# The mixing stage of a hybrid layer: S5 rows loaded and gated first, tiles combined in every other row

## The reference, cut to what matters

```python
w_den = jax.nn.softmax(jnp.stack(lses, axis=0), axis=0)              # 3 groups, per position and head
attn = jnp.einsum('gbsh,gbshd->bshd', w_den, jnp.stack(outs, axis=0))
y_a = attn.reshape(b, s, 512) @ w_attn_proj[l]

y_s = jax.nn.gelu(s5_ssm(...))
y_s = y_s * jax.nn.sigmoid(y_s @ w_glu[l] + b_glu[l])
y_b = y_s @ w_ssm_proj[l]

mixed = jax.nn.sigmoid(gate_a) * y_a + jax.nn.sigmoid(gate_b) * y_b
```

## Time and profile before

| | before |
|---|---|
| median of 3 runs | 5241.57 us (5239.97 to 5242.58) |
| the profiled execution | 5241.3 us, its span 5239.6 us |
| granted TensorE clock over the span | 0.972 |
| TensorE busy | 4959.3 us, 95% of the span |
| VectorE busy | 2979.8 us, 57% |
| ScalarE, GpSimd busy | 1723.3 us, 871.9 us |

### The profile page before, as it was taken

The page is one execution under the profiler, slowest core; times in us unless marked ns, Lnnn a source line. Parts: engine busy times, 40 slices in busy tenths (PEclk is TensorE's granted clock), DMA queues, the critical chain, the costliest instruction groups (busy, mean ns, idle before and its releaser), DMA issues.

```text
span 5239.6 us, 78307 instructions
## 1 busy us (share of the span) xinstructions
PE 4959.3 (95%) x29176; PEld 4413.7 (84%) x29176; DVE 2979.8 (57%) x5537; ACT 1723.3 (33%) x2719; POOL 871.9 (17%) x561
## 2 busy tenths in 40 slices
PE   8999999997689979896999999999999999999998
PEld 6888888886579967685999999999999999999997
DVE  4343331003746666354656666656677777777776
ACT  4121111111246731132333333333334444344443
POOL 0000000002212001133111322213222121222221
PEclk9999999998789989997999999999999999999999
DMA  3222221312244444543454554645566666666665
GB/s 131 77 71 76 88 76 69 113 70 76 42 152 145 148 155 144 173 130 123 168 175 161 170 179 158 202 160 179 181 221 216 222 216 223 240 228 228 226 216 192
DMA packets 254790, 814.55 MB, mean 155 GB/s; under 512 B 33692, under 2 KB 66199, under 8 KB 218136
## 3 DMA queue, kind: packets, MB, share of 16 engines
q1 hardware_dynamic: 218776, 693.78, 36.9%
q0 software_dynamic: 30096, 98.23, 7.7%
q10 hardware_dynamic: 5760, 20.45, 1.2%
HBM read 659.68 MB, written 154.71 MB: 155 GB/s over the span
## 4 chain that ended last, share of the span: by engine, by line
PE 48%; DVE 3%; issue 1%; ACT 0%; DMA 0%; POOL 0%; POOLq 0%; DVEq 0%; ACTq 0%
PE ex_g L2130 31%; PE ex_d L2144 15%; DVE ex_wdl L2237 1%; PE ex_g L2116 1%; DVE ex_xl L2244 1%; ACT ex_xh L2196 0%; DVE ex_at L2267 0%; DVE ex_t L2258 0%; DVE ex_t L2265 0%; DMA ex_nxt<-slots_d 0%; DVE ex_ath L2270 0%; POOL ex_y L2085 0%; DMA ex_xg<-h_d,ex_nxt 0%; DVE ex_y L2285 0%; POOL out L2088 0%
## 5 line engine op out<-in xcount | busy, mean ns | idle before, releaser
L2130 PE MATMUL ex_g<-ex_xh,ex_wgh 128*128 128x256 f32 (+2 forms) x4352 | 1282.9, 295 | 13.7 <-DVE ex_xl L2244 7.4
L2130 PE MATMUL ex_g<-ex_xh,ex_wgl 128*128 128x256 f32 (+2 forms) x4352 | 1276.6, 293 | 0.0
L2130 PE MATMUL ex_g<-ex_xl,ex_wgh 128*128 128x256 f32 (+2 forms) x4352 | 1276.2, 293 | 0.0
L2130 PEld LDWEIGHTS ex_g<-ex_xh,ex_wgh 128*128 128x128 f32 x4352 | 815.8, 187 | 44.0 <-DVE ex_xl L2244 22.0
L2130 PEld LDWEIGHTS ex_g<-ex_xl,ex_wgh 128*128 128x128 f32 x4352 | 816.0, 188 | 7.6
L2130 PEld LDWEIGHTS ex_g<-ex_xh,ex_wgl 128*128 128x128 f32 x4352 | 817.2, 188 | 0.0
L2183 ACT ACTIVATE ex_wgh<-ex_wg 128x2048 fp32r<-128x2048 f32 x274 | 524.5, 1914 | 366.5 <-PE ex_g L2130 340.2
L2231 DVE TENSOR_TENSOR ex_wgl<-ex_wg,ex_wgh 128x2048 fp32r<-128x2048 f32 x274 | 628.7, 2294 | 21.6 <-ACT ex_wgh L2183 16.3
L2085 POOL TENSOR_SCALAR ex_y<-ex_y,ex_cur 128x1024 f32<-128x1024 f32 x82 | 280.3, 3418 | 1552.1 <-DVE ex_y L2285 1552.1
L2144 PE MATMUL ex_d<-ex_wdh,ex_ath 128*128 128x512 f32 x1312 | 523.6, 399 | 0.0
L2144 PE MATMUL ex_d<-ex_wdl,ex_ath 128*128 128x512 f32 x1312 | 515.6, 393 | 0.0
(11 more groups left out here) (375 smaller groups left out, 7838.3 us busy)
## 6 DMA issues: line engine op xcount, KB each, us to landing
ex_wg<-in_w_gu SPq DMA_DIRECT2D x276, 1024.0 KB, 5.1
ex_wd<-in_w_down SPq DMA_DIRECT2D x276, 512.0 KB, 6.1
qkv_d<-prj_o SPq DMA_DIRECT2D x144, 256.0 KB, 2.0
wo_spare<-qkv_d SPq DMA_DIRECT2D x40, 768.0 KB, 4.2
prj_raw<-in_w_in SPq DMA_DIRECT2D x112, 256.0 KB, 3.3
ex_bd<-in_b_down SPq DMA_DIRECT2D x34, 512.0 KB
gate_d<-prj_o SPq DMA_DIRECT2D x64, 256.0 KB, 2.0
mix_ring<-gate_d SPq DMA_DIRECT2D x32, 512.0 KB, 3.9
```

The source lines that it names most:

```text
L2130: last = pe.matmul(gu[j][:, 0:size], w[:, k, j, :], x[:, k, 0:size], start=(k == 0 and x is xh and w is h), stop=(k == KD - 1 and w is l))
```

## The change

The computation stays as it is, instruction for instruction on VectorE; the order changes on all engines.

At the stage's start, the S5 rows are loaded ahead of tile 0, and split first. The GLU of chunk 0 is cut in two halves with the first turn between them. The comparing of tiles 0 and 1 comes ahead of both combinings, and the combinings stand between pairs of gatings. The S5 products of rows 0 and 1 come ahead of the turns of tiles 2 and 3.

In the chunks, the next chunk's tiles are combined in rows 0, 2, 4 and 6 (`COMBINE_AT`), and turned, saved and loaded in rows 1, 3, 5 and 7 (`TURN_AT`). VectorE splits the S5 rows at the head of row 1. The GLU stays behind row 4 (`GLU_AT`), the gatings behind row 5's multiplications; the third save comes behind them. The small tiles of the weights are doubled, so that a tile's comparing can run ahead of the combining of the one before.

In the diff, lines that only add the index `z` to a small tile are left out in `combine`.

```diff
-    STEPS = 8
+    COMBINE_AT, TURN_AT, GLU_AT = (0, 2, 4, 6), (1, 3, 5, 7), 4
...
-        low, den, rden = (t_.sb(n, [P, HG]) for n in ("low", "den", "rden"))
-        dif, wgt, part = (t_.sb(n, [P, NG, HG]) for n in ("dif", "wgt", "part"))
+        low, den, rden = ([t_.sb(f"{n}{z}", [P, HG]) for z in range(2)] for n in ("low", "den", "rden"))
+        dif, wgt, part = ([t_.sb(f"{n}{z}", [P, NG, HG]) for z in range(2)] for n in ("dif", "wgt", "part"))
...
+                load_y(0)
                 load_att(0)
-                load_y(0)
                 load_att(1)
...
-                        if c + 1 < NCH and o < NBLK and NBLK * (c + 1) + o + 2 < NT:
-                            load_att(NBLK * (c + 1) + o + 2)
+                        if c + 1 < NCH and o in TURN_AT and NBLK * (c + 1) + TURN_AT.index(o) + 2 < NT:
+                            load_att(NBLK * (c + 1) + TURN_AT.index(o) + 2)
...
-                def glu(c):
+                def glu(c, parts=range(KA)):
                     z = c % 2
                     pe.wait_ge(yl_ready, c + 1)
-                    for f in range(KA):
+                    for f in parts:
...
+                glu(0, range(KA // 2))
                 turn(0)
-                glu(0)
-                for n in range(1, NBLK):
-                    turn(n)
+                glu(0, range(KA // 2, KA))
+                turn(1)
+
+                product(0, 0, 0)
+                product(0, 1, 0)
+                turn(2)
+                turn(3)
                 for c in range(NCH):
                     more = c + 1 < NCH
                     for o in range(NO):
-                        product(c, o, 0)
-                        if more and 1 <= o < 1 + NBLK:
-                            turn(NBLK * (c + 1) + o - 1)
+                        if c or o >= 2:
+                            product(c, o, 0)
+                        if more and o in TURN_AT:
+                            turn(NBLK * (c + 1) + TURN_AT.index(o))
                         product(c, o, 1)
-                        if more and o == NBLK:
+                        if more and o == GLU_AT:
                             glu(c + 1)
...
-                def gate(c):
-                    for f in range(KA):
-                        act.wait_ge(glu_mm, KA * c + f + 1)
-                        if KA * c + f >= 2:
-                            act.wait_ge(gated, KA * c + f - 1)
-                        act.activation(sg[f % 2][:, :], pg[f % 2][:, :], ACT.Sigmoid, bias=bg[:, f:f + 1]).then_inc(sig, 1)
+                def sigmoid(c, f):
+                    act.wait_ge(glu_mm, KA * c + f + 1)
+                    if KA * c + f >= 2:
+                        act.wait_ge(gated, KA * c + f - 1)
+                    act.activation(sg[f % 2][:, :], pg[f % 2][:, :], ACT.Sigmoid, bias=bg[:, f:f + 1]).then_inc(sig, 1)
+
+                def split_gated(c):
                     act.wait_ge(gated, KA * c + KA)
                     act.activation(flat(yh[c % 2]), flat(y), ACT.Copy).then_inc(y2h_ready, 1)
 
                 def weigh(n):
                     act.wait_ge(dif_ready, n + 1)
-                    act.activation(wgt[:, :, :], dif[:, :, :], ACT.Exp).then_inc(w_ready, 1)
+                    if n >= 2:
+                        act.wait_ge(combined, n - 1)
+                    act.activation(wgt[n % 2][:, :, :], dif[n % 2][:, :, :], ACT.Exp).then_inc(w_ready, 1)
...
+                split_y(0)
                 weigh(0)
-                split_y(0)
+                weigh(1)
                 act.wait_ge(bg_in, 16)
-                weigh(1)
+                sigmoid(0, 0)
+                sigmoid(0, 1)
                 save(0)
-                gate(0)
+                sigmoid(0, 2)
+                sigmoid(0, 3)
+                split_gated(0)
+                save(1)
                 weigh(2)
-                save(1)
                 weigh(3)
                 save(2)
                 save(3)
                 for c in range(NCH - 1):
-                    weigh(NBLK * (c + 1))
-                    for j in range(NBLK):
-                        if j + 1 < NBLK:
-                            weigh(NBLK * (c + 1) + j + 1)
-                        save(NBLK * (c + 1) + j)
-                        if j == 1:
-                            split_y(c + 1)
-                    gate(c + 1)
+                    n = NBLK * (c + 1)
+                    weigh(n)
+                    split_y(c + 1)
+                    save(n)
+                    weigh(n + 1)
+                    save(n + 1)
+                    weigh(n + 2)
+                    for f in range(KA):
+                        sigmoid(c + 1, f)
+                    split_gated(c + 1)
+                    save(n + 2)
+                    weigh(n + 3)
+                    save(n + 3)
...
-                def gate(c):
-                    for f in range(KA):
-                        dve.wait_ge(sig, KA * c + f + 1)
-                        tt(y[:, f, :], y[:, f, :], sg[f % 2][:, :], ALU.mult).then_inc(gated, 1)
+                def gate(c, f):
+                    dve.wait_ge(sig, KA * c + f + 1)
+                    tt(y[:, f, :], y[:, f, :], sg[f % 2][:, :], ALU.mult).then_inc(gated, 1)
+
+                def split_gated(c):
                     dve.wait_ge(y2h_ready, c + 1)
                     tt(flat(yl[c % 2]), flat(y), flat(yh[c % 2]).bitcast(F32), ALU.subtract).then_inc(y2l_ready, 1)
 
+                chain = Steps(dve, step)
+
+                def compare(n):
+                    z = n % 2
+                    dve.wait_ge(a_in[z], 16 * NG * (n // 2) + 16 * NG)
+                    m = [x[:, :, DH] for x in a[z]]
+                    chain(tt(low[z][:, :], m[0], m[1], ALU.min))
+                    chain(tt(low[z][:, :], low[z][:, :], m[2], ALU.min))
+                    for g in range(NG):
+                        last = tt(dif[z][:, g, :], low[z][:, :], m[g], ALU.subtract)
+                    last.then_inc(dif_ready, 1)
+
                 def combine(n):
                     z = n % 2
-                    chain = Steps(dve, step, STEPS * n)
-                    dve.wait_ge(a_in[z], 16 * NG * (n // 2) + 16 * NG)
-                    m = [x[:, :, DH] for x in a[z]]
-                    chain(tt(low[:, :], m[0], m[1], ALU.min))
-                    chain(tt(low[:, :], low[:, :], m[2], ALU.min))
-                    for g in range(NG):
-                        last = tt(dif[:, g, :], low[:, :], m[g], ALU.subtract)
-                    last.then_inc(dif_ready, 1)
                     dve.wait_ge(w_ready, n + 1)
                     for g in range(NG):
-                        last = tt(part[:, g, :], wgt[:, g, :], a[z][g][:, :, DH + 1], ALU.mult)
+                        last = tt(part[z][:, g, :], wgt[z][:, g, :], a[z][g][:, :, DH + 1], ALU.mult)
...
-                    dve.wait_ge(mm, 2 * t + 2)
+                    dve.wait_ge(mm, 2 * t + 2 if t else 3)
...
+                split_y(0)
+                compare(0)
+                compare(1)
                 combine(0)
-                split_y(0)
+                gate(0, 0)
+                gate(0, 1)
                 combine(1)
+                gate(0, 2)
+                gate(0, 3)
                 save(0)
-                gate(0)
+                split_gated(0)
+                save(1)
+                compare(2)
+                compare(3)
                 combine(2)
-                save(1)
                 combine(3)
                 save(2)
                 save(3)
                 for c in range(NCH):
                     more = c + 1 < NCH
                     for o in range(NO):
-                        if more and o == 3:
+                        if more and o == 1:
                             split_y(c + 1)
-                        if more and o < NBLK:
-                            combine(NBLK * (c + 1) + o)
+                        if more and o in COMBINE_AT:
+                            n = NBLK * (c + 1) + COMBINE_AT.index(o)
+                            compare(n)
+                            combine(n)
                         weighed(c * NO + o)
-                        if more and 1 <= o < 1 + NBLK:
-                            save(NBLK * (c + 1) + o - 1)
-                        if more and o == NBLK + 1:
-                            gate(c + 1)
+                        if more and o == GLU_AT + 1:
+                            for f in range(KA):
+                                gate(c + 1, f)
+                            split_gated(c + 1)
+                        if more and o in TURN_AT:
+                            save(NBLK * (c + 1) + TURN_AT.index(o))
```

More of the change, by code:

```diff
@@ L1542, in combine @@
                     dve.wait_ge(w_ready, n + 1)
                     for g in range(NG):
-                        last = tt(part[:, g, :], wgt[:, g, :], a[z][g][:, :, DH + 1], ALU.mult)
+                        last = tt(part[z][:, g, :], wgt[z][:, g, :], a[z][g][:, :, DH + 1], ALU.mult)
                     chain(last)
```

(12 more changed lines are left out.)

## The result

The changed kernel takes 5252.9 us (median of 11 runs, 5251.3 to 5255.7), the one before 5240.5 in the same comparison (11 runs, 5237.2 to 5242.6): 12.4 us more, ratio 1.0026 with a 95% interval of 1.0018 to 1.0035. It is slower, as forecast: the interval lies above 1, though its lower end, 0.18%, lies a little under the 0.2% that the prediction took for what a measurement can tell. Of the 18.3 us that the sum gave, two thirds came.

What follows compares the result with a forecast made beforehand. VectorE bounds wherever a turn stands; what matters is when each tile is combined. Chunks 0 to 2 add +4.5 + 6.3 + 7.5 = +18.3 us on a profiled 5241.3: 5259.9 us, range 5247 to 5267.

Steps and rivals of the forecast that it cites:

- the sum: Chunks 0 to 2 add +4.5, +6.3 and +7.5 us, +18.3 in all, on a profiled 5241.3 us: 5259.9 us.
- Two waits: In chunks 0 to 2, turns waiting for VectorE: near 5 us at the second, near 6.8 at the fourth.
- The start: At the stage's start, the S5 rows land at 1881.7, before at 1884.4; the first product starts at 1906.0, before 1920.85.
- The start's chain on ScalarE and VectorE: From the landing through GLU, gatings and combinings, tiles 2 and 3 are done at 1917.2, against 1920.0 before: 2.8 us earlier.
- Chunk 0's S5 load: Issued at 1920.4, landing after 10.4 us at 1930.8, so the second turn of chunk 0 stands at 1943.3.
- From there to the end of chunk 0: From chunk 0's second turn to its end 48.9 us, so it ends at 1992.2, before at 1987.7: +4.5 us.
- Chunks 1 and 2: S5 rows land at T+12.5 (T: previous chunk's last product ends); chunks of 73.9 us against 67.6 and 66.4.
- and waits 5.0 us: In chunks 1 and 2 TensorE reaches the second turn at T+20.0, the turn starts at T+25.0; the clock falls.
- (a): S5 rows land at T+10.8, wait 3.3 us, clock kept, chunks of 70.0 us: 5252, lower value 5248.5; chance 18%.
- (b): Gatings run beside the GLU, so the fourth turn's wait and clock fall go, 9.1 us per chunk: -9 us; chance 6%.
- (c): VectorE's idle time takes up the moves, no new waits in the chunks: within 2 us, 5242; chance 4%.
- it isn't kept: At the start, TensorE gains two products in the hole from 1906, but stops one product later for tile 4.

Runs made afterwards that it cites:

- the split at row 3: The changed kernel with VectorE's split of the next S5 rows back at the head of row 3: 5233.2 us.
- the old start: The changed kernel's chunks with the start of the kernel before (tile 0 loaded and combined first, all four turns ahead of the first product): 5254.3 us.
- the tile in row 5: The changed kernel with the fourth tile combined at row 5's head, ahead of the gatings: 5235.4 us; with its exponentials behind the second sigmoid, 5229.9 us.
- the start only: The changed kernel's start with the chunks of the kernel before: 5236.9 us.

## Why the prediction held, and where its sizes were off

The direction and the mechanism held, and the sizes did not everywhere. Two waits were forecast, at the second and the fourth turn of chunks 0 to 2; they are there, and each goes by the edit that its cause asks for. The loss is in chunks 1 and 2 alone: chunk 0, for which the sum had +4.5 us, ended 0.5 us earlier than before, because its start and its load were faster than counted. The sum put the start of the last chunk at 2140.0. It was at 2133.1, 6.9 us earlier, and these are the terms:

- The start, -1.7: the S5 rows landed 5.7 us behind their issue, at 1880.0, where I took 1881.7. I had weighed the row of the load that stood behind a tile. The Trainium skill's rule in "DMA: Bandwidth & Descriptors", section "Queues, rings and completion order" (each ring is consumed in order), gave the early end, and the trace agrees with 5.7 us. The other eight traces with this start have 5.7 to 6.7, so a part of this term is the spread between executions.
- The start's chain on ScalarE and VectorE, -1.3: the turn of tile 3 stood at 1914.28 and not at 1917.3. The GLU's quarters came sooner, since the clock rose sooner: its matmuls ran at the lower level for the first 2.7 us, before for 5.3.
- Chunk 0's S5 load, -1.1: it landed after 9.3 us in place of 10.4. So the second turn came at 1939.2 (forecast 1943.3), with a wait of 4.46 us.
- From there to the end of chunk 0, -0.9: 48.0 us against 48.9, for the product behind the turn took 3.8 us, not 4.7.
- Chunks 1 and 2, -1.2 and -0.7: 72.7 and 73.3 against 73.9. The landings were at T+11.65 and T+10.94, forecast T+12.5; both lie between my bounds, T+10.8 and T+13.9. I leaned on the slower row, because as many bytes were ahead. The fourth turn waited 6.6 us (6.8 forecast), in all three chunks.

So the mis-sized term is the landing of the S5 loads: four landings, each taken too late, and 5.3 us of the 6.9 follow from them (1.7, 1.1, 0.9, 1.6); what is left is the clock and the chain of the start. The step "and waits 5.0 us" was 3.9 and 3.2. What I overlooked is that the two waits touch each other. The wait in row 7 also holds back the multiplications behind it, so that the ring load and the store of the row before go out some 3 to 4 us ahead of the last ones, and the S5 load took 7.3 to 8.2 us (this kernel, the split at row 3, the old start). In the two runs with the tile in row 5 and the late load row 7 doesn't wait, only some 0.5 us lie between them, and the load took 8.4 to 9.5, on both sides of the 9.0 that I had taken. No run moves this spacing alone, so that it is the cause is argued, not shown.

Of the rivals, (a) was nearest in time (5252), but not for its reason: it had the clock kept behind a wait of 3.3 us, and it fell behind 3.20 here, and behind 1.99 and 1.86 in later runs. Its chunks of 70 us didn't come. (b) was wrong about the order as written, and near with its price: with the tile taken out from behind the gatings and ScalarE's order mended, the last chunk starts 23.6 us earlier (2109.50), where (b) had 27 for the wait and the clock. With the early load too it is 44 us, and 46.8 in the medians. (c) is out.

In the changed order of the chunks 2.9 us of the start's gain reach the last chunk. That is near the 2.8 that I had counted for it, but by luck: tile 3's turn came 5.8 us earlier (1914.28, before 1920.08), and chunk 0's longer wait gave the rest back. TensorE's own gain, of which I said "it isn't kept", is indeed not kept in that order; in the repaired one, 6.9 us reach the last chunk.

## What to carry to other kernels

An instruction that waits for a transfer holds up everything behind it on its engine; moving it forward in the order needs its load moved forward too. Here either edit alone mended it, the load asked for earlier or the instruction moved back. Work that another engine waits for belongs into the idle stretch ahead of a long dependent chain, not behind it. Here the GLU left VectorE 10.8 us idle ahead of row 5's multiplications (chunk 1 of the kernel after), and the tile that was put behind the gatings fitted in there:

```profile
2037.11 0.69 DVE L1599 TENSOR_TENSOR mix_tb<-mix_o,mix_ring 128x512 f32<-128x512 f32 x1 [10.83 <-issue]
```

When an edit wins less than counted, read the next wait in the trace before doubting the count: the largest missing part of the tile's gain, 4.8 us of 8.8, was ScalarE's order, with exponentials and a table load in front of a sigmoid.

## What the runs showed of the hardware

The clock fell behind shorter waits than the kernel before had shown. It stayed at 1.00 behind 1.84 us, and was 0.61 in the product behind a wait of 1.99 us and 0.65 behind 2.80, while the turn just behind the wait of 1.99 was still short. The run with the start only has both outcomes behind one length of wait. TensorE's rows in chunks 0 and 1, and the product behind the first of them:

```profile
1936.70 0.66 PE L1427 MATMUL mix_t<-k_ident,wo_spare 128*128 128x128 f32 x4 [1.86 <-DVE wo_spare L1585]
...
2003.12 0.66 PE L1427 MATMUL mix_t<-k_ident,wo_spare 128*128 128x128 f32 x4 [1.86 <-DVE wo_spare L1585]
```

```profile
1937.11:1941.54 4.43, 4.43 (x16) 3.47 (x15) 4.39 (x6) 0.00 (x0) 1.28 (x1) 0.61 0.50 134
```

Behind the first wait of 1.86 us the product takes 4.43 us at 0.61; TensorE had waited 1.45 us 8.1 us earlier. Behind the second it takes 2.89 us at 1.00. So a wait's length alone doesn't say whether the clock falls, and I can't say from these runs what does.

How soon a load of 1 MB landed differed with what its queue had just been given. From issue to landing the S5 loads of all twelve traces took:

| issued ahead of the load in SyncE's queue (a pair is a ring load and a store) | loads | us to landing |
|---|---|---|
| in the chunks, nothing for over 4 us | 12 | 5.2 to 5.6 |
| at the stage's start, nothing for 2.5 us, tiles behind it | 9 | 5.7 to 6.7 |
| at the stage's start, three pieces of a tile | 3 | 7.3 to 8.8 |
| a ring load and a store, right behind another such pair | 4 | 6.8 to 7.3 |
| a ring load and a store, some 4 us behind another pair | 2 | 7.0, 7.8 |
| a ring load, a tile and a store, some 3 to 4 us behind another pair | 6 | 7.3 to 8.2 |
| a ring load, a tile and a store, right behind another pair | 4 | 8.4 to 9.5 |
| three ring loads | 8 | 7.9 to 10.4 |

A tile ahead shows plainly at the stage's start and where the pairs stand close; with the pairs apart the ranges with and without it overlap.
